# Experts' input rows fetched as quarter rows and turned by VectorE, hidden values turned one block sooner

## The chip, the cores and the metric

One core of one Trainium2 chip runs the whole program. The metric is the time of one execution on the device in microseconds. Before the change it was 1967.46 us, the median of three runs (1962.0 to 1968.35).

## What is computed

The program is two transformer blocks on 512 tokens of width 1024, all in 32-bit floats. The first block has latent attention beside a state-space branch, cross attention to a memory, and a mixture of experts; the second has a gated unit, sparse attention and a dense feed-forward part. Only the mixture of experts matters here:

```
top8      = router(x2)                          # 8 of 64 experts per token, 512 * 8 = 4096 rows in all
for each expert e, rows x of its tokens (64 on the mean, 96 per pass at most):
    g, u  = split(x @ w_gate_up[e])             # 1024 x 512
    y     = (silu(g) * u) @ w_down[e]           # 256 x 1024
out[token] = shared(x2) + sum over its 8 experts of weight * y
```

Rows beyond 96 of an expert would be done in a second part that runs only if there are any.

## The kernel before, in words

Each engine has its own program, written by hand, and semaphores order them. The experts run one after the other, four to a turn of a loop, with the first and the last four written out.

**Weights.** SP's program loads gate-up as two DMAs of 1 MB (`gate_up_rows`, line 972) and down as one (`down_rows`, line 975), into four buffers each, `gu_w` and `dn_w`; some lie in `ring`, some in slabs. `refill(e, b)` asks for gate-up of expert e + 4 when the gate-up of e is done (`gu_full`), and for down of e + 2 when the last down part of e - 2 is done (`dn2_full`).

**Rows.** The router writes each token's number into a table in HBM, by expert and place. This is `scatter_ids(k)` on POOL (line 3319), four indirect DMAs for each of the token's 8 choices. ACT then brings a column of the table, one per expert, to SBUF as `slot_tok` (`index_column`, line 2044), for the first 8 experts one by one and the other 56 in one DMA (line 2110). POOL's `gather(e)` (line 3330) fetches up to 96 rows of 4 KB of `x2` by it, into `xg[e % 2]`. Places that no token has hold the number 512, which is out of bounds, and nothing is fetched for them. Up to expert 7 POOL's order is `scatter_ids(e + 1)`, `gather(e)`. From expert 2 on, gather e waits until the rows of expert e - 2 have been turned (`xtr_full`).

**Turning.** A product needs the rows with their width along the partitions. PE transposes the 96 x 1024 rows in eight blocks into PSUM (`turn_rows`, line 1438), and ACT copies them to `xe` (`x_copy`, line 2056).

**PE's block for expert e** (`e_block`), in the steady part: turn the hidden values of expert e - 2 (`turn_hidden`, line 1445); turn the rows of expert e + 1 (`turn_next(0)`); wait for `xe`, the weights and the turned hidden values; then eight steps of k, each with gate-up of e in three groups of 32 columns of the array (line 1483) and, in the fourth group, a piece of the down product of e - 2 (line 1491); last the rest of that down product (line 1502).

**ACT** per expert: silu of e - 1 (line 2062), two copies of the last down part (2072), the store of the finished rows of e - 3 into `y_rows` (line 2080), the copies of the turned rows of e + 1, and copies of the first down part (2100). **DVE** per expert: the turned hidden values of e - 2 to `hidT` (`hidden_turned`, line 2799), the gated values of e - 1 (`hidden`, by way of line 2311), two copies (2809, 2810) and two more of the down product (2843). Ahead of its experts DVE finishes the router: weights of the choices, then, up to line 2789, the control words for the second part. Near the end of the experts POOL starts to fetch finished rows back (`slot_rows`, line 3338).

## Time and profile before

| | |
|---|---|
| median of three runs | 1967.46 us (1962.0 to 1968.35) |
| the profiled execution | 1963.43 us |
| its span, first to last instruction | 1961.3 us |
| mean granted clock of PE | 0.987 of full speed |
| PE busy | 1864.2 us (95%) |
| DVE, ACT, POOL busy | 956.7, 523.4, 334.5 us |
| moved by DMA | 375.40 MB, 191 GB/s on the mean |

PE is the fullest engine over the whole span, but the mean covers stages of different kinds. A stage is read from three things: how much of it PE and DMA are busy, what each block of PE waits for, and how long its loads take from issue to landing. The experts are the stretch from about 595 to 1208 us.

### The profile page before, as it was taken

The numbers are of one execution on the slowest core, as the hardware profiler recorded it, in microseconds if no ns is written. First come the engines' busy times: TensorE is split into PE (matmuls) and PEld (weight loads), VectorE is DVE, ScalarE is ACT, GpSimd is POOL, SyncE is SP. The second block draws the span as 40 slices with busy tenths as digits, with TensorE's granted clock in tenths as the row PEclk, the third lists the DMA queues.
The fourth block names the chain that finished last, engine by engine and source line by source line (L and its number), as shares of the span: only waits on it lengthen the run. The fifth ranks groups of instructions, "written<-read, shape, count | busy, mean of one in ns | idle before, by whom it ended". The sixth has DMA issues, their size and how long they took to land. (4 is left out here: it accounts for less than half of the span.)

```text
span 1961.3 us, 28010 instructions
## 1 busy us (share of the span) xinstructions
PE 1864.2 (95%) x10606; PEld 1038.3 (53%) x10606; DVE 956.7 (49%) x2029; ACT 523.4 (27%) x1154; POOL 334.5 (17%) x297
## 2 busy tenths in 40 slices
PE   8999899999998999999999998999999999999997
PEld 3334348854443344444444333457756688888443
DVE  5987748623474233233223325623375554454643
ACT  2448731200211333333333332320264100000000
POOL 0655430000037101001000114400023000000000
PEclk9999999999999999999999999999999999999998
DMA  6114042212356999999999999622310122222411
GB/s 251 64 49 121 22 149 86 86 43 110 151 193 216 377 404 405 400 404 404 406 407 405 399 402 372 233 90 98 129 44 2 43 108 86 86 86 86 138 55 43
DMA packets 80480, 375.40 MB, mean 191 GB/s; under 512 B 13458, under 2 KB 13714, under 8 KB 55184
## 3 DMA queue, kind: packets, MB, share of 16 engines
q1 hardware_dynamic: 55728, 303.59, 40.4%
q10 hardware_dynamic: 11824, 37.02, 5.3%
q0 software_dynamic: 12848, 33.74, 4.7%
q8 instruction: 49, 0.80, 0.2%
q14 instruction: 31, 0.25, 0.0%
HBM read 352.64 MB, written 33.07 MB: 197 GB/s over the span
## 5 line engine op out<-in xcount | busy, mean ns | idle before, releaser
L2843 DVE COPY slab<-bank 32x512 f32<-32x512 f32 x124 | 80.8, 688 | 393.9 <-PE bank L1491 393.9
L1090 PE MATMUL bank<-ring,slab 128*128 128x512 f32 (+1 forms) x608 | 254.3, 578 | 3.6 <-DMA ring<-stream 2.6
L1483 PE MATMUL bank<-slab 128*32 128x512 f32 x1536 | 230.1, 601 | 16.2 <-DVE slab L2799 6.0
L1483 PE MATMUL bank<-ring,slab 128*32 128x512 f32 x1536 | 227.0, 595 | 14.0 <-DVE slab L2799 4.5
L1491 PE MATMUL bank<-ring,slab 128*32 128x512 f32 x512 | 229.6, 602 | 0.0
L1491 PE MATMUL bank<-slab 128*32 128x512 f32 x480 | 212.5, 596 | 0.0
L1090 PEld LDWEIGHTS bank<-ring,slab 128*128 128x128 f32 x608 | 115.9, 192 | 136.4 <-issue 132.0
L3255 POOL TENSOR_TENSOR small<-small 128x1 f32<-128x1 f32 (+2 forms) x30 | 27.5, 921 | 825.3 <-DVE small L2308 825.3
L1090 PE MATMUL bank<-slab,ring 128*128 128x512 f32 (+1 forms) x368 | 148.2, 559 | 2.6 <-ACT slab L1845 1.8
L1483 PEld LDWEIGHTS bank<-slab 128*32 128x32 f32 x1536 | 72.2, 111 | 147.2 <-issue 141.5
L1483 PEld LDWEIGHTS bank<-ring,slab 128*32 128x32 f32 x1536 | 71.2, 110 | 143.8 <-issue 140.6
L3330 POOL DMA_INDIRECT slab<-x_rows,s5x x64 | 61.5, 961 | 480.7 <-PE bank L1438 462.3
L1722 PE MATMUL bank<-work,s5x 128*128 128x256 f32 x528 | 117.4, 379 | 0.0
L1090 PEld LDWEIGHTS bank<-slab,ring 128*128 128x128 f32 x368 | 68.9, 190 | 79.0 <-issue 77.2
L1722 PEld LDWEIGHTS bank<-work,s5x 128*128 128x128 f32 x528 | 100.5, 190 | 13.5
L2311 DVE TENSOR_TENSOR slab<-bank,slab 96x256 f32<-96x256 f32 (+2 forms) x110 | 57.3, 525 | 103.2 <-PE bank L1090 40.2
L2056 ACT ACTIVATE slab<-bank 128x384 f32<-128x384 f32 x128 | 55.8, 488 | 150.5 <-DVE slab L2810 123.4
L2100 ACT ACTIVATE slab<-bank 32x512 f32<-32x512 f32 x124 | 66.6, 584 | 88.1 <-PE bank L1491 88.1
L2311 DVE TENSOR_TENSOR work<-bank,work 128x256 f32<-128x256 f32 x108 | 44.4, 423 | 81.6 <-PE bank L1722 72.0
L1722 PE MATMUL bank<-slab,ring 128*128 128x256 f32 x352 | 79.4, 379 | 0.0
L1722 PEld LDWEIGHTS bank<-slab,ring 128*128 128x128 f32 x352 | 67.0, 190 | 9.4 <-issue 0.5
L2062 ACT ACTIVATE slab<-bank 96x256 f32<-96x256 f32 x64 | 24.3, 379 | 155.8 <-PE bank L1483 142.2
(363 smaller groups left out, 3030.8 us busy)
## 6 DMA issues: line engine op xcount, KB each, us to landing
ring<-stream SPq DMA_DIRECT2D x173, 512.0 KB, 4.4
slab<-w_exp_gu SPq DMA_DIRECT2D x64, 1024.0 KB, 14.0
ring<-w_exp_gu SPq DMA_DIRECT2D x64, 1024.0 KB, 13.6
ring<-w_exp_down SPq DMA_DIRECT2D x32, 1024.0 KB, 22.0
slab<-w_exp_down SPq DMA_DIRECT2D x32, 1024.0 KB, 22.6
y_rows<-slab ACTq DMA_DIRECT2D x64, 384.0 KB, 8.2
y_rows<-zeros ACTq DMA_DIRECT2D x1, 3456.0 KB, 20.5
gb<-rows ACTq DMA_DIRECT2D x5, 512.0 KB, 4.5
```

What stands on the lines that cost most here:

```text
L1090: mm = nc.tensor.matmul(dst, lhs[k], rhs[k], start=(k == 0), stop=(k == len(lhs) - 1))
L1483: mm = nc.tensor.matmul(g_bank[32 * g:32 * g + 32, :], x[:, k, 32 * g:32 * g + 32], w[:, 512 * k:512 * k + 512], start=(k == 0), stop=(k = ...
L1491: mm = nc.tensor.matmul(bank[2 + 3 * t + half][96:128, :], h[:, c * CAP + 32 * t:c * CAP + 32 * t + 32], d[:, c * D + 512 * half:c * D + 5 ...
L1722: mm = nc.tensor.matmul(unit_bank(n, p), w[:, k * P:(k + 1) * P], x[:, k, :], start=(k == 0), stop=(k == 3))
L2056: i = nc.scalar.activation(xe[b][:, 4 * j:4 * j + 4, :], bank[j][:, 0:4 * CAP].rearrange("p (k n) -> p k n", n=CAP), ACT.Copy)
L2062: nc.scalar.activation(gsilu[b], bank[2 + b][0:CAP, 0:FF], ACT.Silu).then_inc(s_ready, 1)
L2100: i = nc.scalar.activation(ye[b % 2][0:32, 512 * half:512 * half + 512], bank[2 + half][96:128, :], ACT.Copy)
L2311: return nc.vector.tensor_tensor(out_, x, y, op)
L2843: i = nc.vector.tensor_copy(ye[b % 2][32:64, 512 * half:512 * half + 512], bank[5 + half][96:128, :])
L3255: nc.gpsimd.tensor_tensor(rstd[:, at:at + w], var[:, at:at + w], minus_half[:, 0:w], ALU.pow).then_inc(rstd_ready, 1)
L3330: pool.indirect_dma_start(xg[e % 2][0:CAP, :], None, scratch["x2"], bass.IndirectOffsetOnAxis(ap=slot_tok[:, e:e + 1].bitcast(U32), axis=0 ...
```

## The change

The rows of an expert are fetched by three indirect DMAs in place of one. Each covers 32 places and all 128 partitions: partition 32q + s gets quarter q (256 values, 1 KB) of the row of place s. So `x2` is addressed as 2048 quarter rows, and the index of a partition is 4 x token + q. POOL works this out on the index table (`row_numbers`, with the new constant `quarter`), and ACT loads each index column four times, once for each quarter of the partitions. VectorE turns the 128 x 768 values in 32 by 32 blocks in one instruction (`rows_turned`), straight from `xg` to `xe`. A step k of the product then contracts over another choice of 128 of the 1024 values, so the host orders the gate-up weights to match. PE's `turn_rows` and ACT's `x_copy` are gone. The buffer `xg` is free again when DVE has turned it (`xe_ready`); DVE turns the rows of e + 1 in its block e, after `gu_full` of e - 1, as `xe` has two halves.

PE turns the hidden values of expert e - 1 in the middle of block e (k = 4), where before it turned those of e - 2 at the start; DVE copies them at that point. The second part for more than 96 rows is changed in the same way and is left out below.

```diff
+QD = D // 4
+CG = CAP // 32
...
-        ctrl_i = s5x[0:1, 3200:3328].bitcast(I32)
-        slot_tok = s5x[0:CAP, 3072:3072 + NE].bitcast(I32)
...
 
-        xg = [slab6[:, 0:1024], slab6[:, 1024:2048]]
-        xe = [slab7[:, b * 1024:b * 1024 + KD * CAP].rearrange("p (k n) -> p k n", k=KD) for b in range(2)]
+        x2q = scratch["x2"].rearrange("t (r n) -> (t r) n", r=4)
+        tab_g = scratch["tab"][0:CAP * PITCH, :].rearrange("(g s e) o -> s g (e o)", g=CG, s=32)
+        xg = [slab6[:, b * CG * QD:(b + 1) * CG * QD] for b in range(2)]
+        xe = [slab7[:, b * 1024:b * 1024 + CG * QD] for b in range(2)]
+
+        def xe_at(b, k, g):
+            return xe[b][:, QD * g + 32 * k:QD * g + 32 * k + 32]
...
-            def turn_rows(b, wait, n, s_free, n_free, s_full):
-                pe.wait_ge(wait, n)
-                if n_free is not None:
-                    pe.wait_ge(s_free, n_free)
-                for j in range(2):
-                    for k in range(4):
-                        mm = nc.tensor.transpose(bank[j][:, k * CAP:(k + 1) * CAP],
-                                                 xg[b][0:CAP, (4 * j + k) * P:(4 * j + k + 1) * P], ident[0:CAP, 0:CAP])
-                mm.then_inc(s_full, 1)
-
...
                 e = 4 * u + b
-                x, w, g_bank = xe[b % 2], gu_w[b], bank[2 + b % 2]
+                w, g_bank = gu_w[b], bank[2 + b % 2]
                 h, d = hidT[b % 2], dn_w[(b + 2) % 4]
                 down = b >= 2 or first > 0
-                if down:
-                    if b >= 3 or first > 0:
-                        pe.wait_ge(ht_ready, e - 2)
-                    turn_hidden(b % 2, hid_ready, e - 1, ht_full)
-                turn_at = TURN_AT[b] if first == 0 else 0 if b < 3 or last > 0 else None
-
-                def turn_next(k):
-                    if k == turn_at:
-                        turn_rows((b + 1) % 2, gathered[(b + 1) % 2], 16 * (2 * u + (b + 1) // 2 + 1), xe_ready, e + 1, xtr_full)
-
-                turn_next(0)
                 pe.wait_ge(xe_ready, e + 1)
                 pe.wait_ge(gu_landed[b], 32 * u + 32)
                 if down:
@@ -1477,10 +1466,10 @@
                     if b >= 3 or first > 0:
                         pe.wait_ge(y0_act, e - 2)
                 for k in range(KD):
-                    if k > 0:
-                        turn_next(k)
+                    if k == 4 and (b >= 1 or first > 0):
+                        turn_hidden((b + 1) % 2, hid_ready, e, ht_full)
                     for g in range(3):
-                        mm = nc.tensor.matmul(g_bank[32 * g:32 * g + 32, :], x[:, k, 32 * g:32 * g + 32], w[:, 512 * k:512 * k + 512],
+                        mm = nc.tensor.matmul(g_bank[32 * g:32 * g + 32, :], xe_at(b % 2, k, g), w[:, 512 * k:512 * k + 512],
                                               start=(k == 0), stop=(k == KD - 1))
                         if k == KD - 1:
                             mm.then_inc(gu_full, 1)
...
                             mm.then_inc((dn0_full, dn1_full)[t], 1)
-                turn_next(KD)
...
                 for b in range(4):
                     e_block(u, b, first=1)
             for b in range(4):
-                e_block(NE // 4 - 1, b, first=1, last=0)
-            pe.wait_ge(ht_ready, NE - 2)
-            turn_hidden(0, hid_ready, NE - 1, ht_full)
+                e_block(NE // 4 - 1, b, first=1)
             pe.wait_ge(ht_ready, NE - 1)
...
-            pe.wait_ge(xe_ready, NE)
...
             def index_column(e):
 
                 act.wait_ge(ids_sent[e], 16 * NT)
-                act.dma_start(slot_tok[:, e:e + 1], tab2[0:CAP, e:e + 1], allow_slow_non_contiguous=True).then_inc(idx_landed[e], 16)
+                for q in range(4):
+                    act.dma_start(x_row[32 * q:32 * q + 32, :, e:e + 1], tab_g[:, :, e:e + 1],
+                                  allow_slow_non_contiguous=True).then_inc(idx_landed[e], 16)
...
-            def x_copy(b, s_full, n_full, s_ready):
-                act.wait_ge(s_full, n_full)
-                for j in range(2):
-                    i = nc.scalar.activation(xe[b][:, 4 * j:4 * j + 4, :],
-                                             bank[j][:, 0:4 * CAP].rearrange("p (k n) -> p k n", n=CAP), ACT.Copy)
-                i.then_inc(s_ready, 1)
...
@@ -2090,8 +2069,6 @@
                 if b >= 3 or steady:
                     y_rest(e - 3, (b + 1) % 2)
                     y_send(e - 3, (b + 1) % 2)
-                if b < 3 or last > 0:
-                    x_copy((b + 1) % 2, xtr_full, e + 2, xe_ready)
                 if b >= 2 or steady:
                     act.wait_ge(dn0_full, e - 1)
                     if steady:
@@ -2101,18 +2078,18 @@
                     i.then_inc(y0_act, 1)
 
...
             index_column(1)
-            x_copy(0, xtr_full, 1, xe_ready)
             index_column(2)
             for b in range(4):
                 e_block(0, b)
                 index_column(b + 3)
             index_column(TOPK - 1)
-            act.dma_start(slot_tok[:, TOPK:NE], tab2[0:CAP, TOPK:NE]).then_inc(idx_rest, 16)
+            for q in range(4):
+                act.dma_start(x_row[32 * q:32 * q + 32, :, TOPK:NE], tab_g[:, :, TOPK:NE]).then_inc(idx_rest, 16)
...
@@ -2809,6 +2785,10 @@
                 nc.vector.tensor_copy(ye[b][64:96, 512:768], bank[4][64:96, 0:256])
                 nc.vector.tensor_copy(ye[b][64:96, 768:1024], bank[4][96:128, 0:256]).then_inc(y2_dve, 1)
 
+            def rows_turned(b, s_got, n_got, s_ready):
...
-                if b >= 2 or steady:
-                    hidden_turned(b % 2, ht_full, e - 1, ht_ready)
                 if b >= 1 or steady:
                     if b >= 3 or steady:
                         dve.wait_ge(ht_full, e - 2)
                     hidden((b + 1) % 2, silu_ready, e, hid_ready)
                 if b >= 3 or steady:
                     y_rest(e - 3, (b + 1) % 2)
+                if not last:
+                    if b >= 1 or steady:
+                        dve.wait_ge(gu_full, 3 * e)
+                    rows_turned((b + 1) % 2, gathered[(b + 1) % 2], 16 * CG * (2 * u + (b + 1) // 2 + 1), xe_ready)
+                if b >= 1 or steady:
+                    hidden_turned((b + 1) % 2, ht_full, e, ht_ready)
                 if slot_ is not None:
                     for t in range(NT):
                         combine(slot_, t)
@@ -2843,6 +2827,7 @@
                         i = nc.vector.tensor_copy(ye[b % 2][32:64, 512 * half:512 * half + 512], bank[5 + half][96:128, :])
...
                 for b in range(4):
                     e_block(u, b, first=1)
             for b in range(4):
-                e_block(NE // 4 - 1, b, first=1, slot_=0 if b == 3 else None)
-            hidden_turned(0, ht_full, NE - 1, ht_ready)
+                e_block(NE // 4 - 1, b, first=1, slot_=0 if b == 3 else None, last=b == 3)
             hidden(1, silu_ready, NE, hid_ready)
             y_rest(NE - 3, 1)
             hidden_turned(1, ht_full, NE, ht_ready)
...
@@ -3319,17 +3304,28 @@
                     pool.indirect_dma_start(scratch["tab"], bass.IndirectOffsetOnAxis(ap=yrow_i[:, 4 * k + t:4 * k + t + 1].bitcast(U32), axis=0),
                                             tok_i[:, t:t + 1], None).then_inc(ids_sent[k], 16)
 
+            rows_made = [0]
+
+            def row_numbers(e0, e1, s_got, n_got):
+
+                pool.wait_ge(s_got, n_got)
+                x = x_row[:, :, e0:e1]
+                nc.gpsimd.tensor_scalar(x, x, 4.0, cst("quarter"), ALU.mult, ALU.add).then_inc(row_ready, 1)
+                rows_made[0] += 1
+                pool.wait_ge(row_ready, rows_made[0])
+
             def gather(e):
                 if e < TOPK:
-                    pool.wait_ge(idx_landed[e], 16)
+                    row_numbers(e, e + 1, idx_landed[e], 64)
                 elif e == TOPK:
-                    pool.wait_ge(idx_rest, 16)
+                    row_numbers(TOPK, NE, idx_rest, 64)
                 if e >= 2:
-                    pool.wait_ge(gathered[e % 2], 16 * (e // 2))
-                    pool.wait_ge(xtr_full, e - 1)
-                pool.indirect_dma_start(xg[e % 2][0:CAP, :], None, scratch["x2"],
-                                        bass.IndirectOffsetOnAxis(ap=slot_tok[:, e:e + 1].bitcast(U32), axis=0),
-                                        bounds_check=T - 1, oob_is_err=False).then_inc(gathered[e % 2], 16)
+                    pool.wait_ge(gathered[e % 2], 16 * CG * (e // 2))
+                    pool.wait_ge(xe_ready, e - 1)
+                for g in range(CG):
+                    pool.indirect_dma_start(xg[e % 2][:, QD * g:QD * g + QD], None, x2q,
+                                            bass.IndirectOffsetOnAxis(ap=x_row[:, g, e:e + 1].bitcast(U32), axis=0),
+                                            bounds_check=4 * T - 1, oob_is_err=False).then_inc(gathered[e % 2], 16)
 
             scatter_ids(0)
             pool.wait_ge(x2_stored, 16 * NT)
...
     }
     arrays = {k: np.ascontiguousarray(v) for k, v in arrays.items()}
...
```

## Rows read from the trace of the kernel before

**Rows 1.** The page, part 2: 40 slices of 49 us, DMA share and GB/s.

```profile
DMA  6114042212356999999999999622310122222411
GB/s 251 64 49 121 22 149 86 86 43 110 151 193 216 377 404 405 400 404 404 406 407 405 399 402 372 233 90 98 129 44 2 43 108 86 86 86 86 138 55 43
```

**Rows 2.** Windows: window, length, each engine's busy us (count), PEclk, DMA share, GB/s.

```profile
580.00:630.00 50.00, 43.08 (x261) 16.78 (x264) 29.36 (x63) 7.04 (x16) 35.74 (x32) 0.97 0.51 164
630.00:660.00 30.00, 27.43 (x266) 10.66 (x259) 7.44 (x17) 8.85 (x21) 8.26 (x9) 0.94 0.95 359
...
700.00:1000.00 300.00, 288.04 (x2912) 125.12 (x2908) 92.86 (x224) 99.67 (x228) 30.61 (x32) 1.00 1.01 404
```

**Rows 3.** Timeline of one steady expert: start, length, engine, line, operation [idle before].

```profile
902.25 0.63 PE L1483 MATMUL bank<-ring,slab 128*32 128x512 f32 x3 [0.43 <-DVE slab L2799]
...
909.12 1.07 PE L1502 MATMUL bank<-slab 128*32 128x256 f32 x16
...
910.12 0.38 PE L1445 MATMUL bank<-const_sb,slab 96*128 96x96 f32 x2
...
910.34 0.82 PE L1438 MATMUL bank<-const_sb,slab 96*128 96x96 f32 x8
...
911.23 0.41 DVE L2311 TENSOR_TENSOR slab<-bank,slab 96x256 f32<-96x256 f32 x1
...
911.52 0.63 PE L1483 MATMUL bank<-ring,slab 128*32 128x512 f32 x3 [0.36 <-issue]
```

**Rows 4.** Line 975 (down weights), windows 650 to 700, then 1000 to 1100.

```profile
DMA to landing us min/median/max: 13.3/14.7/15.2
...
DMA to landing us min/median/max: 26.3/28.5/29.7
```

**Rows 5.** Waits, 650 to 1150 us: waiter <- releaser, total us, times, longest.

```profile
DVE slab L2843 <- PE bank L1491: 341.3, 54, 7.0
...
PE bank L1483 <- DMA slab<-w_exp_down: 3.0, 4, 1.2
```

**Rows 6.** DMA, 700 to 1100 us: queue: packets, MB, share of 16 engines.

```profile
q1 hardware_dynamic: 18316, 133.38, 83.2%
q10 hardware_dynamic: 4816, 16.91, 10.8%
q0 software_dynamic: 4816, 11.42, 7.4%
```

**Rows 7.** DMA, 3 to 4 us: the queue that loads the column table.

```profile
q10 hardware_dynamic: 91, 0.05, 19.1%
```

**Rows 8.** DMA, 600 to 604 us: scatters and a gather.

```profile
q0 software_dynamic: 230, 0.19, 15.3%
```

**Rows 9.** DMA, 908 to 910 us, in the steady part.

```profile
q1 hardware_dynamic: 57, 0.39, 48.0%
q10 hardware_dynamic: 60, 0.23, 30.7%
q0 software_dynamic: 57, 0.17, 21.9%
```

**Rows 10.** Line 3330 (the gathers), 700 to 1100 us.

```profile
DMA to landing us min/median/max: 8.8/9.0/9.6
```

**Rows 11.** Timelines of POOL, PE and DVE at the start of the experts.

```profile
595.43 0.99 POOL L3330 DMA_INDIRECT slab<-x_rows,s5x  x1 [0.31 <-issue]
...
596.82 3.63 PE L1483 MATMUL bank<-ring,slab 128*32 128x512 f32 x24 [0.96 <-ACT slab L2056]
...
607.56 1.54 DVE L2778 TENSOR_REDUCE work<-s5x 1x21 f32<-1x1344 f32 x1
...
660.85 0.63 PE L1483 MATMUL bank<-slab 128*32 128x512 f32 x3 [0.33 <-DVE slab L2799]
```

**Rows 12.** Timeline of PE near the last expert but one.

```profile
1186.76 1.07 PE L1483 MATMUL bank<-slab 128*32 128x512 f32 x3 [3.05 <-DMA ring<-w_exp_down]
```

**Rows 13.** Line 2110 (the rest of the index table).

```profile
DMA to landing us min/median/max: 7.0/7.0/7.0
```

More of the change, by code:

```diff
@@ L461, in host_consts @@
     c["tokid"] = t.astype(f)
+    c["quarter"] = (i // 32).astype(f).reshape(P, 1)
     return c
@@ L897, in build @@
         yf_act, yf_dve = sem("yf_act"), sem("yf_dve")
-        ov = {n: sem("ov_" + n) for n in ("gather", "w", "store", "pe", "act", "dve", "idx", "ygot", "added")}
+        ov = {n: sem("ov_" + n) for n in ("gather", "w", "store", "pe", "act", "dve", "idx", "row", "ygot", "added")}
         home_got = {h: [sem(f"{h}_got{t}") for t in range(NT if h in ("slab1", "ring_lo") else 1)] for h in homes}
@@ L2080, in y_send, with e_block @@
                 act.dma_start(y3[0:CAP, bass.ds(e, 1), :].rearrange("r e d -> r (e d)"), ye[b][0:CAP, :]).then_inc(y_stored[b], 16)
-            def e_block(u, b, first=0, last=NE):
+            def e_block(u, b, first=0):
                 e = 4 * u + b
@@ L2109, in _ @@
             index_column(TOPK - 1)
-            act.dma_start(slot_tok[:, TOPK:NE], tab2[0:CAP, TOPK:NE]).then_inc(idx_rest, 16)
+            for q in range(4):
+                act.dma_start(x_row[32 * q:32 * q + 32, :, TOPK:NE], tab_g[:, :, TOPK:NE]).then_inc(idx_rest, 16)
             with act.Fori(1, NE // 4 - 1) as u:
@@ L2114, in _ @@
             for b in range(4):
-                e_block(NE // 4 - 1, b, first=1, last=0)
+                e_block(NE // 4 - 1, b, first=1)
             act.wait_ge(hid_ready, NE - 2)
@@ L2844, in e_block @@
                     i.then_inc(y1_dve, 1)
+            rows_turned(0, gathered[0], 16 * CG, xe_ready)
             for b in range(4):
@@ L3365, in _ @@
                     with pool.If(n_ov > o):
[L3366 to L3367 removed]
+                        pool.wait_ge(idx_ov, 64 * o + 64)
+                        pool.wait_ge(ov["idx"], 2 * o + 1)
                         nc.gpsimd.tensor_tensor(spare, minus_half[:, 0:1], minus_half[:, 0:1], ALU.mult).then_inc(ov["idx"], 1)
[L3369 to L3371 removed]
+                        nc.gpsimd.tensor_scalar(x_row[:, :, 0:1], x_row[:, :, 0:1], 4.0, cst("quarter"), ALU.mult, ALU.add).then_inc(ov["row"], 1)
+                        pool.wait_ge(ov["row"], o + 1)
+                        nc.gpsimd.tensor_tensor(tiny[:, 5:6], minus_half[:, 0:1], minus_half[:, 0:1], ALU.mult).then_inc(ov["idx"], 1)
+                        for g in range(CG):
+                            pool.indirect_dma_start(xg[0][:, QD * g:QD * g + QD], None, x2q,
+                                                    bass.IndirectOffsetOnAxis(ap=x_row[:, g, 0:1].bitcast(U32), axis=0),
+                                                    bounds_check=4 * T - 1, oob_is_err=False).then_inc(ov["gather"], 16)
                         pool.wait_ge(ov["store"], 16 * o + 16)
```

59 lines of the change are left out of this document (29 added, 30 removed).

## The prediction

> **What bounds the kernel now.** Read the slices of the whole span first: the stage that the change touches is where DMA shows nines, about 590 to 1210 us, the 64 experts [rows 1]. The windows then show PE and DMA together. From 700 to 1000 us PE is busy 288.0 of 300 us, but the 16 DMA engines also stand at a share of 1.01 and move 404 GB/s [rows 2]. Both look full, so the share of busy time settles nothing.
>
> The timeline gives PE's own need. From one expert's first matmul to the next is 911.52 - 902.25 = 9.27 us: 6.87 us of gate, up and part of down, 1.00 us for L1502, 0.22 us for the hidden turn (L1445), 0.82 us for the row turn (L1438), and 0.36 us until the turned hidden values are copied [rows 3].
>
> Whether DMA keeps up is read from how long a down load takes to land: a median of 14.7 us between 650 and 700 us, 28.5 us between 1000 and 1100 [rows 4]. A steady request rate with growing landing times is a queue filling up. It grew by 13.8 us from about 675 to 1050 us, 40 experts, so 0.34 us each: DMA needs 9.27 + 0.34 = 9.6 us per expert, PE 9.27. The four buffers hid this; when they are used up PE starts to wait for w_exp_down (3.0 us in 4 waits by 1150 into slab alone, [rows 5]), and at 1186.76 it waits 3.05 us [rows 12]. At the end PE is behind DMA, and the stage ends when DMA has delivered. A faster PE only brings the waits forward. This is the main point of the prediction.
>
> **Part 1, work taken from PE.** Gone per expert: the row turn, 0.82 us, and the 0.36 us wait, because hidden values of the expert before are turned in mid-block and copied half a block early. The hidden turn itself stays. PE's block is 9.27 - 0.82 - 0.36 = 8.1 us. 52 experts (those after the start) would give 61 us if PE were the bound. It is not: against 9.6 us of DMA, I cost this part at nothing. What takes its place is a wait for weights of some 1.6 us per block. The wait at 1186.76 was followed by matmuls at 1.07 us in place of 0.63 [rows 12, 3]: the granted clock fell to its lower level, 1.2 GHz, after a stand of 3 us. If it falls in every block, a block takes up to 3 us more, PE is then the late one for one block, DMA gets ahead, and the next wait goes. The mean stays DMA's.
>
> **Part 2, work given to DVE and taken from ACT.** ACT loses two copies; it is not on the path. DVE gets one transposition of 128x768. No such operation is in the trace. A DVE product of 96x256 takes 0.41 us [rows 3]; even at three times that for three times the elements it is 1.2 us, and if turning cost three times a copy, 3.7 us. I take 1.0. DVE stands idle 341.3/54 = 6.3 us per expert for PE [rows 5], so all of this range is covered in the steady part; without that cover it would be 64 us. Hidden (L2311) ends at 911.64, and a block begun without the row turn at 910.34 asks for it half of 6.87 us in, at 913.8, so the new wait is met. Rows are turned only after the gate-and-up of the expert before (gu_full), which frees the buffer.
>
> **Part 3, what the gather now costs DMA.** This decides. One DMA of 96 rows of 4 KB becomes three of 128 quarter rows. Of the 96 about 65 are real: 11.42 MB in 43 gathers is 266 KB. The rest, and 16 completion packets per DMA, are empty but issued: 4816 packets in 43 gathers are 112 = 96 + 16 [rows 6]. After: 384 + 48 = 432 packets, 260 of them of 1 KB.
> Packet prices: 4 KB: q0 has 7.4% of 16 x 400 us, 474 us, for 2788 real packets and some 2030 nearly empty ones, 163 ns for a real one [rows 6]. A small loading of 91 packets of 632 B at most (the table of columns) took 19.1% of 16 us, 34 ns each, against 25 ns for 632 B at the rate of the big ones: some 9 ns fixed [rows 7]. Nearly empty packets: 230 q0 packets in 4 us took 9.8 us of engine time, 7.5 of them for 46 real rows, so some 12 ns each for the others, 10 at most when idle time between is left out [rows 8]. So 1 KB is 41 + 9 = 50 ns. Bounds: 41 (no fixed cost; that 8 KB packets take 328 ns, twice a row's 163, speaks for it) and 75 ns (over twice what 632 B took, as these reads are scattered).
> Sum per expert: 260 x 50 - 65 x 163 = 2.4 us of engine time, plus 125 more empty packets x 10 ns = 1.25 us: some 3.6 us over 16 engines, 0.22 us; since the big packets show a smaller fixed cost than the one of 632 B, I take 0.20. With 41 ns it is 0.08 us, with 75 ns 0.63 us. For 52 experts: 10.4 us, bounds 4 and 33.
> The Trainium skill ("DMA: Bandwidth & Descriptors", Specifications) gives 512 B as the size from which a transfer runs at line rate; by it 1 KB pieces would cost no more than whole rows and only the empty packets would add, some 4 us in the sum. The 34 ns for 632 B speak against it: at the rate of big packets they would be 25.
>
> **Part 4, is the gather still in time.** q1, q10 and q0 served 57, 60 and 57 packets in the same 2 us: the engines take one packet of each queue in turn [rows 9]. A gather now lands 9.0 us after issue [rows 10], 7 turns per engine. After it is 27 turns, each behind a weight packet: 83.2% of 6400 us over 16250 data packets are 0.33 us [rows 6]. 27 x (0.33 + 0.05) + 7 turns of the y store x 0.16 = 11.5 us, plus what today's 9.0 us have besides their turns, 9.0 - 7 x 0.65 = 4.4, of which POOL's own issue is part, say 4: 15.5 us. The loop is POOL 0.3, 15.5, DVE 1.0: 16.8 us, and two experts allow 2 x 9.8 = 19.6 us. So I cost it at nothing, but it has only 3 us of room. POOL's three issues are 3 x 1.30 us [rows 11] of 9.8, and overlap it.
> By the Trainium skill ("DMA: Bandwidth & Descriptors", Queues, rings and completion order) an engine drains a packet of 9 to 17 descriptors from one ring before it switches; with that a gather would need few turns and this part would be safe. The row above shows turns of single packets.
>
> **Part 5, the start.** Three things come late. (a) Expert 0's rows: PE starts it at 596.82, but the first turn now stands in DVE's program behind the router's last chain, whose last long step starts at 607.56 and takes 1.54 us, with 1.6 us of small ones and casts behind [rows 11]. With the turn, expert 0 starts at 611.7, 15 us late; PE has stood for that long, so its clock is at the lower level for the first microseconds. (b) Gathers 2 and on wait for the turn of two experts before. POOL's round for experts up to 7 grows from 4 scatters and 1 gather (5 x 1.3 = 6.5) to 4 + 3 issues and the row numbers (0.5, somewhere between 0 and one more issue of 1.3): 9.6 us. (c) Each index column is now four DMAs of ACT, 28 turns per engine where it was 7. The long one took 7.0 us to land [rows 13]; with 21 more turns of 0.34 it takes 14. POOL's round covers about 9 of this.
> Expert 8 started at 660.85 + 2 x 9.27 = 679.4 [rows 11, 3]. With (a) and (b) alone, from 611.7 with rounds of 9.6, the gather of expert 6 is issued near 655 and PE is back at the old times by expert 7, as its blocks are shorter. With (c) at 3 us per expert for experts 4 to 7, and gathers landing up to 6 us later, expert 8 starts near 697. What counts is DMA work not asked for in time: about 4 us in the first case, 16 in the second. I take the middle, 10.
>
> **End.** Down of the last experts lands with DMA, not PE; the last blocks are shorter by 1.2 us, so 1 us less.
>
> **Sum.** 10 + 10.4 - 1 = +19.4 us. The profiled execution took 1963.4 us, 4.1 below the median of the three runs, 1967.5. That gives 1982.8 on its own basis and 1986.9 on the median's; I say 1985. A measurement of this kernel tells 0.3%, 5.9 us, from no change.
>
> **Rivals.**
> (A) DMA bound, but quarter rows and index columns cost next to nothing: start 0 to 4, gathers 0 to 4, end -1: -1 to +7, about 1970. For it: the start has 49% free DMA time between 580 and 630 us, and 5% until 660 [rows 2]. Against it: 34 ns for 632 B. The rule of 512 B in the Trainium skill would lead here. Chance 0.18.
> (B) The gather loop becomes the bound: from 0.53 us per turn in place of 0.43, 27 x 0.53 + 4 + 1.3 = 19.6 us, the loop sets the period. At 0.56 it is 20.4 us, a period of 10.2, so 52 x 0.6 + 9 = +40 us, 2007; at 0.65 it is 11.4 us and +103, 2070. For it: the room of 3 us. Against it: only half of the packets carry data. Chance 0.13.
> (C) Faster: DMA's fullness follows PE's demand and does not limit it. Then PE's 8.1 us decides from expert 8 on: -61 + 10, 1916 us. It needs 404 x 9.27/8.1 = 462 GB/s; no slice of the profile shows over 407 [rows 1], and landing times would not grow. A weaker form is that real rows, always the first 65, load the engines unevenly now, and quarter rows spread over all 128 partitions mend that: 6 rows are 0.98 us on a full engine against 65 x 0.163/16 = 0.66 on the mean, so up to 0.32 less per expert against my 0.20 more: 52 x -0.12 and the start make it 0 to -10. Against it: the share is 1.01 over all 16 engines, none idles. Chance 0.12 for both.
> (D) The forecast, DMA bound and dearer: chance 0.57, its own range 1974 to 2003.
>
> The range for 8 in 10: 1966 to 2010, from the upper half of (A) to the milder (B); out are (C) and the hard (B). Faster 0.12, same 0.18, slower 0.70.
>
> **What the changed profile would show.** PE's block without waits near 8.1 us, but from expert to expert 9.8, with waits of about 1.6 us for DMA ring or slab <- w_exp_down or w_exp_gu from some ten experts after the start; down loads landing after 25 to 30 us all along; DMA share 1.0 and q0 at 432 packets per expert, near 8.4% of the engines; gathers landing near 15 us; DVE's turn near 1.0 us; expert 0 at 611 to 612 us. Wrong would be: a period under 9.4 us (C), waits of PE for the turned rows in the steady part (B), or the stage ending within 5 us of 1208 (A).

## The result, and the profile after

The changed kernel takes 1972.34 us (median of 12 runs, 1969.0 to 1976.38), the kernel before 1967.45 us (median of 12, 1962.0 to 1969.11). The ratio is 1.0032, 95% interval 1.0022 to 1.0043: slower by 0.3%. The profiled executions have spans of 1970.2 and 1961.3 us, 8.9 us apart. The direction of the forecast was right and the time lies in its range, but of the +19.4 us of the sum only 5 to 9 came. That is not one term that was a bit too large: two terms were wrong, with errors of opposite sign.

The page of the changed kernel, part 2, the DMA lines of the 40 slices; they answer to [rows 1]:

```profile
DMA  6114042213354799999999999704310122222311
GB/s 250 64 48 121 22 148 86 89 40 110 150 192 160 266 414 414 414 415 415 415 415 414 415 415 380 262 27 154 135 44 1 43 105 89 86 86 86 128 64 43
```

Two things are to be seen. The slices 13 and 14 (590 to 690 us), where the experts begin, fell from 216 and 377 to 160 and 266 GB/s. And every full slice rose, from 404 to 414. The windows say the same beside the engines (window, length, busy us of PE, PEld, DVE, ACT, POOL with counts, granted clock, DMA share, GB/s); they answer to [rows 2]:

```profile
580.00:630.00 50.00, 32.09 (x147) 11.42 (x149) 29.79 (x60) 0.98 (x2) 37.56 (x36) 0.83 0.37 121
630.00:660.00 30.00, 21.98 (x190) 6.28 (x178) 6.89 (x14) 3.65 (x8) 17.04 (x19) 0.89 0.86 311
660.00:700.00 40.00, 32.58 (x312) 10.66 (x316) 16.55 (x34) 9.91 (x23) 17.08 (x20) 0.87 0.74 274
...
700.00:1000.00 300.00, 277.01 (x2726) 89.46 (x2718) 132.86 (x267) 72.53 (x165) 99.22 (x100) 1.00 1.02 414
```

GB/s times length, summed from 580 to 700 us, is 26.3 MB after and 35.0 MB before: 8.7 MB not asked for in time, 21 us at 414 GB/s. After 700 us the queues gain 10 GB/s on some 490 us, 4.9 MB or 12 us. The difference, +9 us, is what the end shows. The last block of the stage is read from the small group of down that closes each block (L1502 before, L1490 after), here of experts 4, 17, 61 and 63 in the changed kernel:

```profile
673.12 0.60 PE L1490 MATMUL bank<-slab 128*32 128x256 f32 x8
...
779.49 0.61 PE L1490 MATMUL bank<-slab 128*32 128x256 f32 x8
...
1190.03 0.61 PE L1490 MATMUL bank<-slab 128*32 128x256 f32 x8
...
1215.68 0.61 PE L1490 MATMUL bank<-ring,slab 128*32 128x256 f32 x8
```

```profile
649.14 0.60 PE L1502 MATMUL bank<-slab 128*32 128x256 f32 x8
...
1181.66 0.64 PE L1502 MATMUL bank<-slab 128*32 128x256 f32 x8
...
1205.76 0.64 PE L1502 MATMUL bank<-ring,slab 128*32 128x256 f32 x8
```

The second fence is the kernel before, experts 4, 61 and 63. Expert 4 came 24.0 us late. From there to expert 17 the blocks took (779.49 - 673.12)/13 = 8.18 us against 9.27 and won 14 us back. Then the weights were the bound: (1190.03 - 779.49)/44 = 9.33 us per block. The end is 9.9 us late.

What PE waits for, 560 to 1250 us (waiter <- releaser, total us, times, longest), for [rows 5]:

```profile
PE bank L1472 <- DMA ring<-w_exp_down: 28.9, 24, 3.4
PE bank L1472 <- DMA slab<-w_exp_down: 18.4, 22, 1.2
PE bank L1472 <- DVE slab L2790: 17.9, 1, 17.9
PE bank L1445 <- DVE slab L2287: 11.8, 3, 8.7
PE bank L1472 <- DVE slab L2775: 6.3, 1, 6.3
```

The first two lines are the steady part, 1.0 us per block, as the forecast had it in kind. The other three are the start: the first expert's turn, the hidden values of expert 3 in the middle of a block, and late turned hidden values.

The DMA queues, 700 to 1100 us (packets, MB, share of 16 engines), for [rows 6]:

```profile
q1 hardware_dynamic: 18775, 136.71, 83.2%
q10 hardware_dynamic: 4928, 17.30, 10.6%
q0 software_dynamic: 6425, 11.75, 7.9%
```

44 experts went by in this time, so q0 has 146 packets per expert, 48 of them completions (16 for each DMA, as in [rows 6]). The forecast had 432. The 1 KB pieces are not packets of their own: the other 98 packets carry 267 KB, and the places without a token are among them. The first line says more: q1, the weights, has 83.2% of the engines as before [rows 6], but moves 136.71 MB in place of 133.38. So the gain does not show as idle engine time put to use; the same weights take 2.4% less of it. They land sooner too, after 6.1 us where whole rows took 9.0 [rows 10]; the view of L3326 over the whole kernel says:

```profile
DMA to landing us min/median/max: 2.1/6.1/8.9
```

The start, on three engines. DVE and PE at expert 0:

```profile
608.31 1.54 DVE L2754 TENSOR_REDUCE work<-s5x 1x21 f32<-1x1344 f32 x1
...
611.58 1.81 DVE L2790 STREAM_TRANSPOSE slab<-slab 128x768 f32<-128x768 f32 x2
...
612.79 1.07 PE L1472 MATMUL bank<-ring,slab 128*32 128x512 f32 x3 [17.91 <-DVE slab L2790]
```

And ACT, DVE and PE around expert 4, by time:

```profile
650.70 0.98 DVE L2790 STREAM_TRANSPOSE slab<-slab 128x768 f32<-128x768 f32 x1 [8.64 <-DMA slab<-x_rows,s5x]
...
652.36 1.07 PE L1472 MATMUL bank<-ring,slab 128*32 128x512 f32 x3 [6.32 <-DVE slab L2775]
...
653.42 10.82 ACTq L2029 DMA_DIRECT2D s5x<-slot_table  x8
664.26 1.90 ACTq L2087 DMA_DIRECT2D s5x<-slot_table  x4
666.46 0.38 ACT L2041 ACTIVATE slab<-bank 96x256 f32<-96x256 f32 x1 [22.81 <-issue]
...
666.94 0.42 DVE L2287 TENSOR_TENSOR slab<-bank,slab 96x256 f32<-96x256 f32 x1 [13.48 <-ACT slab L2041]
...
667.42 0.58 PE L1445 MATMUL bank<-const_sb,slab 96*128 96x96 f32 x2 [8.74 <-DVE slab L2287]
```

Read the second from the bottom. PE stood 8.74 us in the middle of expert 4's block, for hidden values; these waited for the silu of expert 3; ACT had been ready since 643, but in its program the index columns 6 and 7 stand ahead of that silu, and these wait for POOL's scatters (22.81 us). Before the change the hidden turn stood at the head of a later block, where a late silu hurt less. The row at 652.36 also shows matmuls of 1.07 us where 0.63 is usual: the granted clock is lower after the stands, 0.83 in the window from 580 to 630 us and 0.89 until 660, against 0.97 and 0.94 [rows 2]. Ten steps of k in expert 4's block took 0.85 us in place of 0.43, so of the 28.1 us from the close of expert 3's block to the close of expert 4's some 4 are the clock.

### The profile page after: what moved, and what is told of

It is laid out like the page before. It is cut to its first block and busy times, and to the rows that moved or that the text cites. A ratio compares the mean times of both kernels' runs of the same rounds, so it can differ in the third digit from the quotient of the medians.

```text
span 1970.2 us, 27149 instructions
## 1 busy us (share of the span) xinstructions
PE 1830.0 (93%) x10094; PEld 965.4 (49%) x10094; DVE 1023.3 (52%) x2093; ACT 467.0 (24%) x1026; POOL 466.4 (24%) x434
## 5 line engine op out<-in xcount | busy, mean ns | idle before, releaser
L1472 PE MATMUL bank<-ring,slab 128*32 128x512 f32 x1536 | 238.4, 608 | 42.6 <-DMA slab<-w_exp_down 18.4
L3326 POOL DMA_INDIRECT slab<-x_rows,s5x x192 | 194.5, 1013 | 352.2 <-DVE slab L2790 288.3
L1472 PE MATMUL bank<-slab 128*32 128x512 f32 x1536 | 235.4, 601 | 28.9 <-DMA ring<-w_exp_down 28.9
L1480 PE MATMUL bank<-ring,slab 128*32 128x512 f32 x512 | 234.5, 601 | 0.0
L1480 PE MATMUL bank<-slab 128*32 128x512 f32 x480 | 221.5, 605 | 0.0
L1472 PEld LDWEIGHTS bank<-ring,slab 128*32 128x32 f32 x1536 | 61.9, 112 | 178.0 <-issue 173.4
L1472 PEld LDWEIGHTS bank<-slab 128*32 128x32 f32 x1536 | 60.9, 110 | 160.7 <-issue 137.1
L2775 DVE COPY slab<-bank 128x96 f32<-128x96 f32 x128 | 27.0, 252 | 109.8 <-PE bank L1445 109.7
```

Of the source, the lines that this page charges most:

```text
L1472: mm = nc.tensor.matmul(g_bank[32 * g:32 * g + 32, :], xe_at(b % 2, k, g), w[:, 512 * k:512 * k + 512], start=(k == 0), stop=(k == KD - 1))
L1480: mm = nc.tensor.matmul(bank[2 + 3 * t + half][96:128, :], h[:, c * CAP + 32 * t:c * CAP + 32 * t + 32], d[:, c * D + 512 * half:c * D + 5 ...
L2775: i = nc.vector.tensor_copy(hidT[b][:, j * CAP:(j + 1) * CAP], bank[7][:, j * CAP:(j + 1) * CAP])
L3326: pool.indirect_dma_start(xg[e % 2][:, QD * g:QD * g + QD], None, x2q, bass.IndirectOffsetOnAxis(ap=x_row[:, g, e:e + 1].bitcast(U32), axi ...
```

## The experiments

Each kernel is measured against the kernel before on the same chip. Two theories were at stake from the start: that the steady part gained because quarter rows load the DMA engines evenly (the weaker form of rival (C)), and that the loss is all in the first experts.

**Only the order of the places (x1, x14).** Kernel before, whole rows, but the 96 places of an expert laid over the partitions so that the some 65 real ones are no longer the first 65 partitions. The results are stored back from the same places:

```
+tab_s = scratch["tab"][0:CAP * PITCH, :].rearrange("(i j e) o -> j i (e o)", j=16, e=PITCH)
+y_s = scratch["y"][0:CAP * PITCH, :].rearrange("(i j e) d -> j i e d", j=16, e=PITCH)
-act.dma_start(slot_tok[:, e:e + 1], tab2[0:CAP, e:e + 1], ...
+act.dma_start(slot_tok[:, e:e + 1], tab_s[:, :, e:e + 1], ...
```

> The kernel before, whole rows and PE's turn as they are, but the 96 places of an expert are laid on the partitions in another order: partition 6j + i gets place 16i + j, in the index table's loads and in the stores of the results. Theory 1 (uneven engines): the real rows are always the first 65 or so, and if each DMA engine serves 6 neighbouring partitions, engines 0 to 10 carry all of them; laid out evenly, DMA needs 9.3 us per expert as in the changed kernel and no longer 9.6, PE's 9.27 us is the bound to the end, no waits for w_exp_down from 1085 us on, the last block ends near 1197 instead of 1205.8, and the time falls by 7 to 10 us (ratio 0.995 to 0.9965). Theory 2 (it is the quarter rows, or PE reading less, that made DMA faster): nothing changes, 0.999 to 1.001.

Measured: 1958.03 us against 1967.99, ratio 0.9938 (0.9919 to 0.9957). A second series, beside a later kernel:

> x1 a second time, on the same chip as x13, so that the two can be compared: 1956 to 1960.

It gave 1954.5 us, a little below what was expected, against 1965.29, ratio 0.9952 (0.9939 to 0.9966). From 880 to 1160 us, the kernel before and then this one:

```profile
880.00:1160.00 280.00, 265.99 (x2692) 114.15 (x2688) 87.07 (x210) 91.56 (x210) 28.70 (x30) 1.00 1.01 404
```

```profile
880.00:1160.00 280.00, 268.87 (x2717) 116.70 (x2713) 87.14 (x210) 93.19 (x212) 28.77 (x30) 1.00 1.02 410
```

404 became 410 GB/s from nothing but which partition a row comes to and leaves from, blocks stay at 9.28 us (to the end in x14, but for the last three in x1), and the waits for weights are gone. The weights' queue, 700 to 1100 us, shows the same gain as the changed kernel's, 135.28 MB in 82.4% of the engines:

```profile
q1 hardware_dynamic: 18574, 135.28, 82.4%
```

That the order of the places is worth some 6 GB/s is shown, twice. That it is by loading the 16 engines evenly is the reading that led to the experiment, and it is not shown: no view splits the load by engine, and the mean share hardly moves (1.01, 1.02).

**What set PE's 9.27 us (x2, x3).** Kernel before with the loop that turns rows cut (PE turns 2 of 8 blocks, so six blocks of the rows are missing from the product), with the places as they were and then spread:

```
                for j in range(2):
-                    for k in range(4):
+                    for k in range(1):
```

> The kernel before, but PE turns only 2 of the 8 blocks of an expert's rows (the rest of the turned rows is left over from earlier, so the output is not the reference's). PE's block falls from 9.27 to about 8.66 us. Theory DMA bound: the blocks run at 8.7 us until the buffers are used up, by 800 us, then at 9.6 us, and the last ends within 4 us of before's 1205.8; time -4 to +1 us. Rival PE bound: 8.7 us to the end, about -35 us.

> Both edits: places spread evenly over the partitions, and PE turns only 2 of the 8 blocks (same part left out). Theory 1 (uneven engines): DMA bound at 9.3 us per expert in place of 9.6 once the buffers are used up, 0.3 us for some 50 experts, so 12 to 18 us less than x2_short. Theory 2: the same as x2_short within 3 us.

Measured: 1969.5 and 1957.87 us (one run each), 11.6 us apart, just short of theory 1's 12 to 18. In both the blocks stay at 9.27 us, which no theory had said, though 0.6 us of PE's work is gone; the first is then bound by the weights at (1156.35 - 1004.08)/16 = 9.52 us from expert 42 on, the second is not before expert 60. So the row turn was not what filled the block. The next block's start waits for VectorE's copies of the turned hidden values (the wait for L2799 in [rows 3]), and these come behind other copies in VectorE's program; the row turn only lay in that gap.

**Each part of the change alone (x8, x12).** Quarter rows with the hidden turn back at the head of the block (the changed kernel with this; VectorE's copies go back with it):

```
+                if down:
+                    if b >= 3 or first > 0:
+                        pe.wait_ge(ht_ready, e - 2)
+                    turn_hidden(b % 2, hid_ready, e - 1, ht_full)
...
-                    if k == 4 and (b >= 1 or first > 0):
-                        turn_hidden((b + 1) % 2, hid_ready, e, ht_full)
```

> One part of the change alone: quarter rows turned by VectorE stay, and the hidden values are turned at the head of the next block but one again, as before the change. Theory 1 (the chain over VectorE at the head of the block set the block of 9.27, not PE's work, and the gap of 28 us at expert 4 came from PE reaching the hidden turn in the middle of its block while ScalarE stood in a wait): blocks of 9.2 to 9.35 us from expert 5 to the end, no catching up after the start; but the gap at expert 4 is 8 us or more shorter; time 1955 to 1968. Rival (PE's removed row turn of 0.82 us was what made the block shorter, the moved hidden turn nothing): blocks of 8.2 to 8.5 us until the DMA queues are the bound, and the time is 1968 to 1976, as the whole change's.

Measured: 1974.16 us, ratio 1.0043 (1.0032 to 1.0054). Blocks of 9.27 us to the end, as theory 1 said, though PE turns no rows at all; the time stands in waits for the copies of the turned hidden values (700 to 1250 us):

```profile
PE bank L1474 <- issue: 29.6, 30, 1.0
PE bank L1474 <- DVE slab L2779: 27.1, 26, 1.0
```

From the close of expert 3's block to that of expert 4's are 21.8 us in place of 28.1. The total did not come out, it lies 6 us above its interval. I had taken a good part of the start's loss for the hidden turn's, and most of it is the quarter rows': 27.1 MB moved from 580 to 700 us, hardly more than the changed kernel's 26.3. Then the kernel before with the opposite edit, the hidden turn moved and nothing else:

> The other part of the change alone: the kernel before, whole rows turned by PE, with the hidden values turned one block sooner, in the middle of the block. Theory 1 (the hidden turn's place is what held PE's block at 9.27, and the DMA queues at 9.5 to 9.6 us per expert are next): blocks of 8.9 to 9.1 us while the weights are ahead, then 9.55 to 9.65 us to the end, as in x10; no loss in the start; time 1965 to 1971, the same as before within 0.2%. Rival (the row turn and the hidden turn only help together): blocks of 9.27 us as long as in the kernel before, until 1085 us.

Measured: 1976.12 us, ratio 1.0053 (1.0035 to 1.0071), 5 us above its interval and no better than the whole change. Blocks of 9.13 us and later 9.5 to 9.6 us, as expected, but "no loss in the start" was wrong: expert 5 closes its block at 669.10 us, 10.7 later than before, with 32.5 MB moved by 700 us in place of 35.0. PE now stands in mid-block for hidden values (L1445) that it had met ready, 4.3 us of it in the start (560 to 1250 us):

```profile
PE bank L1445 <- DVE slab L2307: 7.0, 2, 4.3
```

The rest of the 10.7 us was not taken apart. So either part alone gives 0 or 0.14 us per block, and both together 1.09. Both cost the start.

**The start repaired (x6, x7).** The changed kernel, with expert 0's rows turned ahead of the router's chain, and ACT's index columns moved behind the silus that they held up:

```
+            dve.wait_ge(gathered[0], 16 * CG)
+            nc.vector.transpose(xe[0], xg[0]).then_inc(xe_ready, 1)
...
-                index_column(b + 3)
+                if b < 3:
+                    index_column(b + 3)
+            e_block(1, 0, first=1)
+            index_column(6)
+            e_block(1, 1, first=1)
```

> The changed kernel with its start mended in two places: the turn of expert 0's rows stands in DVE's program ahead of the router's last chain, and ACT waits for the index columns 6 and 7 only after the silu of experts 3 and 4. Theory (the loss is at the start): PE starts expert 0 near 600 instead of 612.8 and expert 4's down part ends near 657 instead of 673; DMA is asked for 10 to 15 us of work sooner, and the time falls to 1957 to 1962. Rival (POOL's round of 13 us for scatters and gathers holds the start whatever the other engines do): less than 4 us gained, 1968 to 1972.

Measured: 1977.56 us, ratio 1.0049 (1.0032 to 1.0066), no better, and above both intervals. Expert 0 starts at 598.03 us, 14.8 earlier, and expert 4's block closes at 663.54, 9.6 earlier; but column 6 is now issued at 659.88 and POOL stands for it, then for column 7:

```profile
669.18 0.27 POOL L3320 TENSOR_SCALAR s5x<-s5x,const_sb 128x3 int32<-128x3 int32 x1 [15.32 <-DMA s5x<-slot_table]
...
683.15 0.27 POOL L3320 TENSOR_SCALAR s5x<-s5x,const_sb 128x3 int32<-128x3 int32 x1 [9.21 <-DMA s5x<-slot_table]
```

The loss had only been moved, to experts 6 and 7 (700.26 against 697.66 us). With column 6 in its old place and only column 7 late:

```
+            e_block(1, 0, first=1)
             index_column(TOPK - 1)
```

> The changed kernel with two edits in its start: VectorE turns expert 0's rows ahead of its router chain, and ScalarE fetches index column 7 and the remaining 56 columns only after the silu of expert 3 (column 6 stays in its old place, unlike in x6). Theory 1 (the 24 us that the changed kernel lost by expert 4 are waits of in-order engines on late index columns and late rows; x6 only moved the wait to column 6): the last group of down of expert 4 starts near 655 us and that of expert 7 near 691, the DMA queues lose 8 to 14 us of work less than in the changed kernel, and the time falls to 1958 to 1966. Rival (column 7 has the same trouble as column 6 had: POOL needs it for expert 7's rows by 668, and it lands late): POOL waits 9 us or more for it, expert 7 comes at 700, and the time is 1971 to 1978, as x6's. PE's blocks in the steady part stay 9.3 us by both.

Measured: 1964.61 us, ratio 0.9987 (0.9976 to 0.9997). The time is theory 1's, 8 us below the changed kernel, though experts 4 and 7 come at 661.14 and 696.21 us, later than it said (655 and 691): what went with the time are the bytes moved, 29.4 MB by 700 us in place of 26.3, and 3.1 MB are 7.5 us. POOL's longest wait for a column is 7.0 us. It still falls 5.6 MB short of the kernel before.

**Are quarter rows as such cheaper or dearer (x10, x9)?** PE made fast enough (hidden turn moved, 2 of 8 row blocks turned, so six are missing from the product) for the weights to be the bound, with whole rows in their old places and spread:

> As x9 but with the rows in their old places (engines loaded unevenly): hidden values turned one block sooner, and PE turning 2 of the 8 blocks of the rows (six of eight row blocks are missing from the product). Against x2, which has the short row turn alone and kept blocks of 9.27 us until 1004 us. Theory 1 (the hidden turn at the head of the block, behind VectorE, held PE at 9.27): blocks of 8.3 to 8.7 us in the first part, then 9.5 to 9.55 us once the weights are the bound, and a time of 1966 to 1972, no better than x2's 1969.5. Rival (the hidden turn's place is worth nothing): 9.27 us again until 1004, and as x2 throughout.

> The kernel before with three edits: whole rows laid over the partitions so that all DMA engines carry the same (x1), the hidden values turned one block sooner, and PE turning only 2 of the 8 blocks of each expert's rows (so six of eight row blocks are missing from the product). PE's block is then short enough for the DMA queues to be the bound, with whole rows. Theory 1 (quarter rows cost and gain nothing in DMA but evenness): in the DMA-bound part the blocks take 9.25 to 9.35 us, as the changed kernel's 9.29 to 9.31. Rival A (1 KB pieces cost something that evenness hides): 9.05 to 9.2 us. Rival B (quarter rows are cheaper by themselves, since they leave in packets of 4 KB): 9.45 to 9.55 us. Time by theory 1: 1940 to 1952.

Measured: 1970.24 and 1964.25 us (one run each); the second lies 12 us above theory 1's 1952. Blocks of 8.64 us first in both: two edits that give 0 and 0.14 us alone take 0.63 off together. Then the pace that the weights set, over experts 26 to 58: 9.63 us in the old places, 9.48 spread, and 9.33 in the changed kernel. The spread places give 0.15 of the 0.30; the other 0.15 is theory 1's miss, and leans to rival B (9.45 to 9.55): quarter rows are no dearer, perhaps cheaper. That a whole row is a coarse grain (one more row on an engine is 0.16 us) and that the spread y store takes 11.0% of the engines where it took 10.7 (880 to 1160 us) may be part of it; this was not separated. But the short row turn itself is a rival for it. x3 has the spread places and the short turn with x1's blocks of 9.27 us, and moves no more than x9: from 880 to 1160 us it has 405 GB/s at a share of 1.02, where x1 has 410 and x9

```profile
880.00:1160.00 280.00, 256.69 (x2478) 85.35 (x2474) 87.33 (x205) 91.02 (x207) 27.74 (x29) 1.00 1.02 406
```

So some 4 GB/s, 0.09 us of the 0.15 as an estimate (1% of 9.4), seem to go with leaving out part of the turn and not with whole rows. x3 and x9 are one run each, and why it should be so, no run shows.

**The best of both (x11, x13).** Spread whole rows with the hidden turn moved, first everywhere, then only from expert 3 on:

```
-                e_block(0, b)
+                e_block(0, b, head=True, mid=False)
+            for b in range(4):
+                e_block(1, b, first=1, head=b == 0)
```

> x1 (whole rows laid over all DMA engines) with the hidden values turned one block sooner. x1 ran blocks of 9.285 us to the end without a DMA wait, x9 was held by the DMA queues at 9.48 us. Theory U (the 9.48 of x9 is what whole rows cost once PE runs ahead and keeps more transfers open, however short PE's own block is): blocks of 8.9 to 9.1 us first, then 9.4 to 9.5 us; time 1959 to 1965, 1 to 7 us above x1's. Theory V (x9's rate came from its shortened row turn, and the queues give one expert in 9.28 us as in x1): 8.9 to 9.1 first, then 9.25 to 9.3; time 1953 to 1958, the best of all.

> x11 with the hidden values of experts 0 to 2 turned at the head of the block as in the kernel before, and one block sooner only from expert 3 on. Theory (turning sooner costs the start 7 to 8 us, because PE then waits in the middle of a block for silu and hidden while ScalarE and VectorE are held by late index columns and rows; expert 5 came at 666.0 in x11 and 658.4 in the kernel before): expert 5 near 658 to 660, blocks of 9.13 us after that until the weights are the bound, some 10 blocks earlier than in x11, last block 1195 to 1200; time 1951 to 1958, 3 to 9 us below x11's. Rival (the queues give 410 GB/s at most and lost nothing in x11's start, so blocks that come sooner only wait longer): expert 5 earlier, last block 1200 to 1203 as in x11 and x1; time 1957 to 1962.

Measured: 1960.92 us for the first (0.9967, 0.9951 to 0.9982; runs from 1951.03 to 1964.69), and 1952.37 us for the second (0.9934, 0.9921 to 0.9947; 1951.51 to 1954.54). x11's time is theory U's, but its blocks met neither theory: they stay at 9.13 us until expert 61, without 9.4 or 9.28. An estimate reconciles the two. Where the weights are the bound, an expert's transfers come to 9.33 us x 415 GB/s = 3.87 MB in the changed kernel and 9.48 us x 406 GB/s = 3.85 MB in x9. At x11's 411 GB/s that is 9.4 us, 0.24 to 0.29 more than its block, so over 56 experts PE uses up 13 to 16 us of loads made ahead. The changed kernel used up (9.33 - 8.18) x 13 = 15 us before it met its bound. The reserve of x11 and x13 just lasts to the end of the stage; by the same estimate x1's queues need some 9.4 us per expert too, and only the reserve keeps its 9.28.

The second is the fastest kernel of the study, 2 us below x1 on the same chip with intervals that overlap, and its marks came as written, but for the bound, which it never met: expert 5 at 659.33, the last block at 1195.45 us:

```profile
659.33 0.61 PE L1506 MATMUL bank<-slab 128*32 128x256 f32 x8
...
1195.45 0.61 PE L1506 MATMUL bank<-ring,slab 128*32 128x256 f32 x8
```

**All kernels in two numbers.** If the stage ends when DMA has delivered, its end follows from the MB moved from 580 to 700 us and the GB/s after that (700 to 1190 us). The kernel before needs 35.0 MB + 505.8 us x 404 GB/s = 239.3 MB; the rest is computed from that:

| kernel | MB by 700 us | GB/s after | last block by this | measured |
|---|---|---|---|---|
| before | 35.0 | 404 | (basis) | 1205.8 |
| changed | 26.3 | 414 | 1214.4 | 1215.7 |
| x8, quarter rows only | 27.1 | 410 | 1217.7 | 1217.2 |
| x12, hidden turn only | 32.5 | 403 | 1213.2 | 1216.1 |
| x6 | 26.4 | 413 | 1215.6 | 1215.1 |
| x7 | 29.4 | 414 | 1206.9 | 1208.2 |
| x2 | 35.2 | 403 | 1206.5 | 1210.7 |
| x3 | 35.1 | 406 | 1202.9 | 1199.2 |
| x10 | 34.4 | 402 | 1209.7 | 1210.6 |
| x9 | 33.5 | 407 | 1205.6 | 1205.0 |
| x1, spread | 34.8 | 409 | 1200.0 | 1200.2 |
| x11 | 32.9 | 411 | 1202.3 | 1202.2 |
| x13 | 34.9 | 412 | 1196.2 | 1195.5 |
| x14, spread again | 35.4 | 410 | 1197.3 | 1197.7 |

The rows from which the changed kernel's and x13's rates come:

```profile
700.00:1190.00 490.00, 448.62 (x4400) 144.84 (x4396) 212.83 (x429) 117.57 (x267) 166.21 (x167) 1.00 1.02 414
```

```profile
700.00:1190.00 490.00, 485.32 (x4766) 174.48 (x4762) 158.92 (x371) 162.48 (x371) 63.72 (x66) 0.99 1.02 412
```

Eleven kernels end within 3 us of it, two within 4.2 (x2 and x3). It must nearly close, as all kernels load the same weights: it is an account of bytes, not yet a cause, and where PE sets the pace (x8, x1), the GB/s is what it asks for. What it shows is where each kernel won and lost, in the start or in the rate.

## Why the prediction was wrong

It forecast +19.4 us and +5 to +9 came. That the time still lies in the range is luck: two terms were off by 22 and 11 us, one each way. The time lies below (D)'s own 1974 to 2003 and next to rival (A)'s 1970, but (A)'s start of 0 to 4 us was wrong as well, and the sign written down for (C), a period under 9.4 us, is the one that came.

**The bound** was right. PE's waits in the changed kernel are for down weights, PE is busy 277 of 300 us where it was 288, and the stage ends with the weights. The prediction's 9.6 us per expert for the old layout came out: the kernel before takes (1181.66 - 1085.61)/10 = 9.6 us once its reserve is used up.

**Part 1** was right in its size: 8.18 us against 8.1, worth nothing in the sum. It was wrong in what it took the pieces from, -0.82 for the row turn and -0.36 for the wait, as if each could be had alone: x2, x8 and x12 show 0, 0 and 0.14 us alone. The waits that took its place are 1.0 us and not 1.6, and the granted clock, which might have fallen in every block, stayed at 1.00 from 700 to 1190 us.

**Part 2**: 0.98 us for the turn against 1.0, hidden in the steady part.

**Part 3 is the step that failed**, "+0.20 us, 52 experts, 10.4 us", which the prediction called the one that decides. Two things in it were wrong. Its count: 146 packets per expert, not 432. So the price is 7.9% of 16 x 400 us over 44 experts, 11.5 us of engine time, against 11.0 before [rows 6]: 0.03 us per expert over 16 engines. The price of a packet was not the fault: the few packets of 1036 B that q0 has from 700 to 1100 us took 50 ns on the mean in the trace, as forecast. I had assumed a packet for every quarter row. And its sign: the gain by evenness was there, worked out under rival (C) as 0.32 us per expert, and set aside with "the share is 1.01 over all 16 engines, none idles". The pace in the DMA-bound stretch went from 9.6 to 9.33 us, 0.27 less. x1 shows that another order of whole rows gives 6 of the 10 GB/s; that evenness is how, and what the other 4 are, stays open. In place of +10 the term is -12 to -14. The rule of the Trainium skill ("DMA: Bandwidth & Descriptors", Specifications), that transfers of 512 B and more run at line rate, gave the better sum here: by it whole and quarter rows cost the same.

**Part 4** was right in its verdict, not in its numbers: landing in 6.1 us, not 15.5; the loop had much room. Here the Trainium skill's rule on draining a packet of several descriptors before switching ("DMA: Bandwidth & Descriptors", Queues, rings and completion order) goes the right way: some 260 pieces left in 98 packets, though that is a few to a packet and not the 9 to 17 that the page gives. [rows 9] counts packets and can't tell how many pieces one holds, so it spoke neither for nor against.

**Part 5** failed in size. (a) came out: expert 0 at 612.79 us against 611.7. (b) did not: the first gathers start at 591.07, 602.91, 614.13, 625.62, 638.97 and 652.47 us, 12.3 us apart and not 9.6, since a round also has the row numbers' hand-over (0.27 us and 0.80 of wait), single issues of 1.6 to 2.6 us and, in the last two rounds, waits of 3.5 us for the index column. Expert 8 starts about 698.8 us, near the 697 of the worse case, but the DMA work lost is 21 us, beyond its 16. What was missing is the chain over ACT: I had not asked what is queued behind ACT's wait for columns 6 and 7 (the silu of expert 3), nor that the hidden turn in mid-block now makes PE wait for it. The term is +21, not +10. x7 bears this out: with the start in part repaired, 7.5 us of it came back.

**The sum** by what was measured: 21 - 12 = +9 us on the profiled span (+8.9); the runs' ratio gives +6. The forecast (D) had the right mechanism, DMA bound, with a price of the wrong sign; the weak form of (C), put at a part of 0.12, is what the steady part does in size; its time was missed because the start took back more than it gave.

## What to carry to other kernels

In a stage bound by DMA, count two things: bytes not asked for while the stage starts, and what the real rows of a gather with skipped indices do to the rate where they all lie in the first partitions; a mean DMA share of 1.0 does not show the second, and laying the places out over the partitions cost nothing here. Before moving a wait into the middle of a block, follow it back over every in-order engine at the start of the loop, where the producers are late. A step that only fills another chain's gap is worth nothing until that chain is cut too, so cut both or neither.

## What the runs showed of the hardware

The DMA engines of this kernel at a share of 1.01 to 1.02 moved between 399 GB/s (x10, 880 to 1160 us) and 415 GB/s (the changed kernel). The order of the places is one reason (404 against 409 and 410 in x1 and x14), but not the only one: x10, with the old order, moved 412 GB/s from 700 to 770 us, while weights were ahead, and 401 from 780 to 1000. The 1 KB elements of an indirect gather share packets: 98 packets carry 267 KB, and three gathers of 128 quarter rows land in 6.1 us where one of 96 whole rows takes 9.0. VectorE turns 128x768 values in blocks of 32 by 32 in 0.98 us. The spread layout of whole rows gives 405 to 407 GB/s in x3 and x9, which turn 2 of 8 row blocks, and 409 to 412 in x1, x14, x11 and x13, which turn all; PE's pace is not what parts them, as x3's blocks are 9.27 us and x11's 9.13. Why a shorter row turn should slow the queues stays open.
